# Expert results weighted on VectorE and scattered to rows by choice and token

## What is computed

```
gates = sum over both choices of one_hot(expert) * w_sel          # w_sel: softmax of the two, times p_group
acc   = acc + gate[:, e] * ((silu(t @ w1[e]) * (t @ w3[e])) @ w2[e])  # for e in 0..31
x     = x + g2 * acc                                              # g2: one row for context, one for latent tokens
y     = x * rsqrt(mean(x * x) + eps) * final_norm_g
```

## Time and profile before

| | |
|---|---|
| median of 3 runs | 724.87 us (724.36 to 725.55) |
| the profiled execution | 726.14 us, of which the span of the trace is 724.2 us |
| mean granted clock of TensorE | 0.922 |
| busy: PE, DVE, ACT, POOL | 597.5, 260.8, 165.0, 113.3 us |
| moved by DMA | 182.52 MB, 252 GB/s over the span |

### The profile page before, as it was taken

How to read it: one execution, slowest core, us unless ns; L and a number is a source line. 1 busy time by engine, 2 the same in 40 slices (tenths; PEclk the granted TensorE clock), 3 DMA queues, 4 the chain that set the end, 5 groups by cost and what they waited for, 6 DMA issues and landing times.

```text
span 724.2 us, 8452 instructions
## 1 busy us (share of the span) xinstructions
PE 597.5 (82%) x3472; PEld 396.5 (55%) x3472; DVE 260.8 (36%) x529; ACT 165.0 (23%) x306; POOL 113.3 (16%) x89
## 2 busy tenths in 40 slices
PE   3799999999999899999997469998888888787400
PEld 3579999888888644544554445554444444443100
DVE  1441248350504443515677627321111111111067
ACT  5333531122221322201111112111111111111143
POOL 0134623333332000010000011010000000000140
PEclk9899999999999999999999569999999999989855
DMA  7985133033032698379106829999999999998273
GB/s 284 387 305 175 40 117 117 0 117 115 2 117 81 245 354 307 119 257 350 60 30 251 330 78 377 423 422 421 422 419 423 419 421 420 422 423 347 63 276 145
DMA packets 50001, 182.52 MB, mean 252 GB/s; under 512 B 5445, under 2 KB 5493, under 8 KB 37161
## 3 DMA queue, kind: packets, MB, share of 16 engines
q1 hardware_dynamic: 37688, 150.78, 52.9%
q0 software_dynamic: 6192, 20.15, 7.8%
q10 hardware_dynamic: 6080, 11.02, 4.3%
HBM read 170.89 MB, written 14.19 MB: 256 GB/s over the span
## 4 chain that ended last, share of the span: by engine, by line
PE 63%; DMA 21%; DVE 7%; SPq 3%; ACT 3%; issue 2%; ACTq 0%; POOL 0%; DVEq 0%; POOLq 0%
DMA ring<-in_w_up_e 13%; PE bank L924 9%; PE bank L926 9%; PE bank L925 9%; PE bank L1094 9%; PE bank L1170 9%; DMA arena_ab<-in_w_up_e 5%; PE bank L1190 4%; PE bank L883 3%; DMA x<-in_x_sample 1%; PE bank L1111 1%; PE bank L1162 1%; SPq L447 1%; SPq L443 1%; PE bank L1044 1%
## 5 line engine op out<-in xcount | busy, mean ns | idle before, releaser
L1170 PE MATMUL bank<-ring,arena_ab 128*64 128x256 f32 x416 | 111.7, 430 | 30.1 <-DMA ring<-in_w_up_e 28.7
L1174 PE MATMUL bank<-ring,arena_ab 128*64 128x256 f32 x416 | 111.7, 430 | 0.0
L1170 PEld LDWEIGHTS bank<-ring,arena_ab 128*64 128x64 f32 x416 | 62.9, 155 | 83.0 <-DMA ring<-in_w_up_e 42.4
L1264 DVE TENSOR_TENSOR arena_ab<-arena_ab,bank 64x256 f32<-64x256 f32 x32 | 19.5, 610 | 193.1 <-ACT arena_ab L812 193.1
L533 POOL TENSOR_TENSOR w_lo<-ring,w_hi 128x1024 fp32r<-128x1024 f32 x25 | 61.3, 2454 | 112.5 <-ACT w_hi L672 112.5
L924 PE MATMUL bank<-xn_hi,w_hi 128*128 128x320 f32 x192 | 61.5, 320 | 3.2 <-DVE xn_lo L1264 3.1
L924 PE MATMUL bank<-w_hi,xn_hi 128*128 128x512 f32 x160 | 63.2, 395 | 0.0
L1174 PEld LDWEIGHTS bank<-ring,arena_ab 128*64 128x64 f32 x416 | 62.9, 155 | 0.0
L925 PE MATMUL bank<-w_lo,xn_hi 128*128 128x512 f32 x160 | 62.8, 393 | 0.0
L926 PE MATMUL bank<-w_hi,xn_lo 128*128 128x512 f32 x160 | 62.8, 392 | 0.0
L926 PE MATMUL bank<-xn_hi,w_lo 128*128 128x320 f32 x192 | 60.1, 313 | 0.0
(11 more groups left out here) (223 smaller groups left out, 873.4 us busy)
## 6 DMA issues: line engine op xcount, KB each, us to landing
ring<-in_w_gate_e SPq DMA_DIRECT2D x26, 1024.0 KB, 26.1
ring<-in_w_up_e SPq DMA_DIRECT2D x26, 1024.0 KB, 29.0
ring<-in_w_down_e SPq DMA_DIRECT2D x26, 1024.0 KB, 28.1
ring<-in_w_ada SPq DMA_DIRECT2D x11, 2048.0 KB, 12.2
ring<-in_w_in SPq DMA_DIRECT2D x6, 2048.0 KB, 8.4
expert_out_rows<-arena_ab ACTq DMA_DIRECT2D x64, 128.0 KB, 7.1
arena_ab<-in_w_gate_e SPq DMA_DIRECT2D x6, 1024.0 KB, 27.9
arena_ab<-in_w_up_e SPq DMA_DIRECT2D x6, 1024.0 KB, 30.5
```

Source lines behind the costliest of these rows:

```text
L1170: pe.matmul(bank[2 + p_][0:BLK, 0:DE], lhs, w_gate(s)[:, kt, :], start=(kt == 0), stop=(kt == KT - 1))
L1174: last = pe.matmul(bank[2 + p_][BLK:2 * BLK, 0:DE], lhs, w_up(s)[:, kt, :], start=(kt == 0), stop=(kt == KT - 1))
L1264: return dve.tensor_tensor(out, in0, in1, op)
```

## The change

The result of a slot is now weighted where it leaves PSUM, and only used slots are written, to a row that is the token's own.

- VectorE works out the weights right after the index list (`weights` before the first expert; the inputs of the exponentials are sent to ScalarE before the last `place`). `out_tags` writes for each token and expert a tag (token number, plus 640 for the second choice) and the weight. `out_table` on TensorE multiplies the one-hot slot matrices by these and so gets, for each slot, its destination row and its weight, apart for context and latent tokens. `out_rows` turns that into `row_out`, the list of half rows to write to (out of range for empty slots), and `g_ctx`, `g_lat`.
- For each expert VectorE's `gate_rows` makes a tile `gate_row` = g2 of the latent tokens times the slot's latent weight plus g2 of the context tokens times its context weight, and `results` multiplies the down product by it out of PSUM. ScalarE's `results` is gone.
- POOL scatters the tile by an indirect DMA to `half_rows`: 2 x 2 x 640 half rows of 512 numbers, by choice, token and half. A scatter waits for `y_ev`.
- In the tail SyncE loads both choices of a tile by two contiguous DMAs, `combine` is two sums, `first_part` is gone. The load of the final norm's weights stands behind the last scatter on POOL's queue.
- `result_rows` and its list are gone; the copy of g2 in SBUF is by halves (`second_gate`).

```diff
@@ def rows_back / gathers on POOL
             for q_ in range(PAIRS):
...
+            def result_rows_out(n, p_, column):
+                pool.wait_ge(y_ev, n + 1)
+                pool.indirect_dma_start(half_rows, bass.IndirectOffsetOnAxis(ap=column, axis=0), ysb[:, p_, :], None,
+                                        bounds_check=2 * 2 * TOK - 1, oob_is_err=False).then_inc(y_out[p_], 16)
+            for q_ in range(2):
+                gather_rows(q_, idx[:, q_:q_ + 1])
+            pool.wait_ge(row_out_ready, 1)
+            for m in range(PAIRS):
+                if m + 2 < PAIRS:
+                    pool.wait_ge(xe_mm, 2 * (m + 1))
+                    gather_rows(m % 2, idx[:, m + 2:m + 3])
+                for p_ in range(2):
+                    result_rows_out(2 * m + p_, p_, row_out[:, 2 * m + p_:2 * m + p_ + 1])
             pool.dma_start(g_fin, a["final_norm_g"].partition_broadcast(P)).then_inc(gfin_in, 16)
...
-            for t in range(NT):
-                for j in range(2):
-                    result_rows_in(t, j, y_rows[0:OV_ROW0, :], OV_ROW0 - 1).then_inc(got_in[t], 16)
@@ sync
             sp.sem_inc(y_all, 1)
+            for t in range(NT):
+                for j in range(2):
+                    sp.dma_start(got[:, t, j, :], y_rows[j * TOK + P * t:j * TOK + P * t + P, :]).then_inc(got_in[t], 16)
@@ scalar
-            def results(n, p_, stored_before):
-                act.wait_ge(down_mm, n + 1)
...
-                act.activation(ysb[:, p_, :], bank[6 + p_][:, :], ACT.Copy).then_inc(y_ev, 1)
...
-            def first_part(t):
-                act.wait_ge(got_in[t], 32)
-                act.activation(got[:, t, 0, :], got[:, t, 0, :], ACT.Copy, scale=wsel[:, t, 0:1]).then_inc(part0_ready, 1)
@@ tensor
+            def out_table():
+                pe.wait_ge(tags_ready, 1)
+                for t in range(NT):
+                    cols = slice(2 * EXPERTS * min(t, 1), 2 * EXPERTS * min(t, 1) + 2 * EXPERTS)
+                    for j in range(2):
+                        for half in range(2):
+                            last = pe.matmul(bank[6][BLK * half:BLK * half + BLK, cols], hit(t, j), tag_out[:, t, j, :],
+                                             start=(t < 2 and j == 0), stop=(t in (0, NT - 1) and j == 1))
+                last.then_inc(table_mm, 1)
+            out_table()
             def rows_T(p_, tiles):
...
                 pe.wait_ge(ht_ready, n + 1)
+                if n == 0:
+                    pe.wait_ge(row_out_ready, 1)
@@ vector
             choose(NT - 1)
+            tt(rt[:, 60:65], rt[:, 170:175], rt[:, 165:170], ALU.subtract).then_inc(exp_in, 1)
             place(NT - 1)
...
+            def gate_rows(p_, lat, ctx_):
+                then(dve.tensor_scalar(gate_row[:, p_, :], second_gate[:, 1, :], lat, None, ALU.mult))
+                then(dve.scalar_tensor_tensor(out=gate_row[:, p_, :], in0=second_gate[:, 0, :], scalar=ctx_, in1=gate_row[:, p_, :],
+                                              op0=ALU.mult, op1=ALU.add))
+            def results(n, p_):
+                dve.wait_ge(down_mm, n + 1)
+                if n >= 2:
+                    dve.wait_ge(y_out[p_], 16 * (n // 2))
+                tt(ysb[:, p_, :], bank[6 + p_][:, :], gate_row[:, p_, :], ALU.mult).then_inc(y_ev, 1)
...
             row_table()
-            tt(rt[:, 60:65], rt[:, 170:175], rt[:, 165:170], ALU.subtract).then_inc(exp_in, 1)
+            weights()
+            out_tags()
+            out_rows()
...
+                if n >= 1:
+                    results(n - 1, (n - 1) % 2)
+                gate_rows(n % 2, g_lat[:, n:n + 1], g_ctx[:, n:n + 1])
                 if n == 0:
                     overflow_counts()
-                elif n == 1:
-                    result_rows()
...
                 g0, g1 = got[:, t, 0, :], got[:, t, 1, :]
                 dve.wait_ge(got_in[t], 32)
-                dve.wait_ge(part0_ready, t + 1)
-                then(dve.scalar_tensor_tensor(out=g0, in0=g1, scalar=wsel[:, t, 1:2], in1=g0, op0=ALU.mult, op1=ALU.add))
-                then(tt(g0, g0, rows[3][:, min(t, 1), :], ALU.mult))
+                then(tt(g0, g0, g1, ALU.add))
                 tt(x[:, t, :], x[:, t, :], g0, ALU.add).then_inc(x2_ready[t], 1)
```

More of the change, by code:

```diff
@@ L1229, in _ @@
                 pe.wait_ge(ht_ready, EXPERTS)
+                pe.wait_ge(ov_tags_ready, 1)
+                for n in range(2 * NT):
+                    lo = 64 * (1 + min(n // 2, 1))
+                    for half in range(2):
+                        pe.matmul(bank[5][BLK * half:BLK * half + BLK, lo:lo + 2 * OVB], hit_ov[:, n, :], tag_ov[:, n, :],
+                                  start=(n in (0, 2)), stop=(n in (1, 2 * NT - 1)))
                 for n in range(2 * NT):
@@ new lines, in weights, with out_tags @@
+                then(tt(w_sel[:, :, 1], w, e21, ALU.mult))
+            def out_tags():
+                mine = b_ada_all[:, 128:128 + 2 * NT * EXPERTS].rearrange("p (t j n) -> p t j n", t=NT, j=2)
+                choices = [te(flat2(CHOICE[j])) for j in range(2)]
+                dve.tensor_copy(tag_out[:, :, 0, 0:EXPERTS], mine[:, :, 0, :])
+                dve.scalar_tensor_tensor(out=tag_out[:, :, 1, 0:EXPERTS], in0=choices[1], scalar=float(TOK), in1=mine[:, :, 1, :],
+                                         op0=ALU.mult, op1=ALU.add)
+                for j in range(2):
+                    last = tt(tag_out[:, :, j, EXPERTS:2 * EXPERTS], choices[j], over(w_sel[:, :, j], EXPERTS), ALU.mult)
+                last.then_inc(tags_ready, 1)
@@ new lines, in _ @@
+                ov(dve.scalar_tensor_tensor(out=tag_ov.rearrange("p (t j) b -> p t j b", j=2)[:, :, 1, 0:OVB],
+                                            in0=on.rearrange("p (t j) b -> p t j b", j=2)[:, :, 1, :], scalar=float(TOK), in1=second,
+                                            op0=ALU.mult, op1=ALU.add), 3)
+                tt(on, on, over(rt[:, 240:250], OVB), ALU.mult).then_inc(ov_tags_ready, 1)
+                dve.wait_ge(ov_slot_mm, 1)
+                token, none = rt[:, 300:300 + OVB // 2], rt[:, 320:320 + OVB // 2]
@@ L1705, in _ @@
+                ov(dve.tensor_copy(token, bank[4][:, 0:OVB // 2]), 4)
+                ov(dve.tensor_scalar(none, token, 0.0, float(FAR), ALU.is_equal, ALU.mult), 5)
                 dve.scalar_tensor_tensor(out=idx_ov[:, :], in0=token, scalar=-1.0, in1=none, op0=ALU.add,
                                          op1=ALU.add).then_inc(idx_ov_ready, 1)
[L1707 to L1713 removed]
+                dest, empty = rt[:, 340:340 + OVB], rt[:, 370:370 + OVB]
@@ L1716, in _ @@
+                dve.wait_ge(ov_rows_ready, 1)
             dve.wait_ge(gfin_in, 16)
-            dve.wait_ge(rows_in[3], 16)
             dve.wait_ge(routed, 1)
```

148 lines of the change are left out of this document (79 added, 69 removed).

## The result

The changed kernel took 716.04 us (median of 6 runs, 711.56 to 721.61) beside 725.53 us (6 runs) of the kernel before: ratio 0.9878, 95% interval 0.9833 to 0.9923, so 9.5 us faster. A later comparison gave 717.53 us (715.34 to 724.31) beside 726.31, ratio 0.9899 (0.9861 to 0.9938). The forecast was 713.8, with a range from 707.5 to 718.5.

A forecast was written before the change was run, and what follows sets the result against it. The prediction took the DMA engines as the bound from about 440 us, then one chain from the last expert to the end. Its terms, 0.2 + 0.3 - 3 - 8.6 = -11.1 us, took 724.87 to 713.8, range 707.5 to 718.5.

The forecast's parts named there:

- Start, +0.5 us in all: Start of the expert stage: +0.2 us for new weight and table work, +0.3 for two more VectorE operations at expert 0.
- rival 2: Start of the stage: the table takes 5 us, not hidden by the gather; +2 to +3 us, 716.5; chance 0.08.
- DMA-bound stretch, -3 us: Expert stage from about 440: writing only used slots relieves the slowest DMA engine; 3 us saved, bounds 0 and 7.
- rival 1: DMA-bound stretch: the scatter relieves all DMA engines alike, 7 us in place of 3, so 709.8; chance 0.18.
- the drain: End of the weights, as DMA engines finish at different times: up to 8 us before, 10 us or more forecast.
- the ring: Middle of the expert stage: loop of product, scatter, gather, transposes and down product, forecast at 16.1 us for two experts.
- Tail, -8.6 us: Behind the last expert: 2.1 us sooner to the first loaded results, then 6.5 us from one VectorE operation less per tile.
- rival 4: No effect in the middle and the final norm's weights late: 720; chance 0.14 together with the mild form.
- rival 3: Middle, on POOL: gathers wait behind scatters; mild 716 to 723 (0.14 together with rival 4), full 750 (0.05).
- That makes 16.1, below 17.2: Middle: loop of 5.6 us plus 10.5 for the gather's landing, compared with gathers 17.24 us apart before.
- the mild form: Rival 3 with a gather landing near 12 us: 716 to 723; chance 0.14 together with rival 4.
- backlog of the DMA queue: Middle: a later TensorE only shortens this backlog; with the loop as bound, the queue empties and landing falls towards 4.3 us.

The follow-up runs named there:

- the gathers ahead: Changed kernel with POOL issuing the gather of pair m+3 before the two scatters of pair m instead of behind them; 712.06 us, ratio 0.9819.
- all rows written: Kernel with the gathers ahead, each unused slot scattered to a spare row of its own instead of skipped; 714.41 us, ratio 0.9841.
- the spread: Kernel with the gathers ahead, consecutive slots dealt to partitions four apart; 705.63 us. Same edit in the kernel before 725.69, in the changed kernel 711.85.

## Why the prediction was right in its time and wrong in its path

**What bounds the kernel.** The DMA engines as the bound from 440 on: true before and with the gathers ahead (a share of 1.01 in 440 to 480 and 1.02 in 480 to 640 in both), not in the changed kernel (0.99 in 440 to 480, and 14 waits on gathered rows).

**Start, +0.5 us in all: nothing.** The table took 2.45 us (priced 2.6, 419.06 to 421.51) and was hidden by the gather. The index list ended 0.5 us sooner in this execution, at 417.24; counted from there the first copy of transposed rows came after 6.4 us, as in the earlier trace rows, and the first expert's gate and up products, at 425.31, after 8.1, as before. So rival 2 is out.

**DMA-bound stretch, -3 us: the size holds, the place does not.** The saved rows are worth 3.5 us of the weights' landing in one pair of profiles and 2.4 us of the medians once the weights are the bound (all rows written), so rival 1, with 7, is out. The slowest engine was the better choice than the mean byte: the spread, at the same bytes, brings the landing forward by another 4.1 us, and the drain with the gathers ahead is 13 us, longer than the 8 before, as the prediction said. That weights and old stores load all engines evenly rests on the mean share of 1.01 to 1.02 from 440 to 640, not on a view of each engine; with only the gathers' slots spread, in the kernel before, the drain went from 8 us to 3. In the time of the changed kernel none of the 3 us was seen, for TensorE had the ring to wait for.

**Tail, -8.6 us: right, a little small.** From the end of the last transposes to the end of the span 9.6 us went: 1.55 from ScalarE's hidden state (1.5 priced), 6.3 from the two sums per tile (6.5 priced), and 1.75 between the last product and the first sum (0.6 priced). There the scatter landed 2.4 us after POOL began it and not 4.3, and the first tile's loads took 6.9 us from the first issue, where 6.1 was priced with the norm's share. The first three final norms are 4.21 us apart, 5.53 before, the 1.3 closer that the prediction named. VectorE did not wait for the final norm's weights, so that half of rival 4 is out; its other half, no effect in the middle, is what came.

**The step that failed is rival 3's sum**, "That makes 16.1, below 17.2", by which the ring was set aside and the mild form got a part of 0.14. Three things were wrong in it.

First the comparison. 17.24 us is the pace of gathers after 488. Up to there the kernel before ran at 12.34 us a pair, and the ring held these early pairs back as well: its first three turns took 17.7, 18.0 and 16.8 us. The ends had to be compared, not two paces. First gather 449.55, 12 turns of 16.1, 9.9 for the last landing, and 25.2 from there to the end of the last down product (four experts at 6.17 and little else): 677.9. That is already 2 us later than the 675.9 which the forecast had for the last down product's end. With the measured 16.61 it is 684.0, the 683.98 of the trace, as it must be with all terms from there.

Second a term of the sum. The transposes and the down product were priced at 2.6 us, with the down product of the earlier trace rows, where the granted clock was 1.00 (678 to 680.5). In the ring they took 4.2 in the turn shown and 3.8 in the mean of 13, behind waits of TensorE. The gather was priced too high in return: it landed after 9.7 in the mean, not 10.5. With the other steps as measured (0.1 more) that makes 16.6 where 16.1 was forecast, so this term is worth less than the comparison. With a quick product the ring was 14.5 to 15.2 us long, and the same sum with 14.8 ends at 662, ahead of the 673.9 at which the weights let the last down product end with the gathers ahead; with the slow products the ring is the bound. That is worked out and was not run.

Third the argument that a shorter "backlog of the DMA queue" or an emptier queue would give the loss back. The DMA share in 440 to 480 fell only from 1.01 to 0.99, and a gather still took 9.5 us to land.

The price at a granted clock of 1.00 did not hold for most turns: it was 0.50 in 660 to 662 after no matmul in 656 to 658, and 0.51 to 0.65 over the slow products of the first profile, 0.50 to 0.64 over those of the second. But 2 of 13 turns in the first profile and 5 of 13 in the second had a quick product, at 1.00. A lower clock behind the waits was not weighed against rival 3.

So 716.04 came out where the tail's 9.6 is nearly all of the gain and the middle gave nothing, with 2.2 us between forecast and median, and a single execution anywhere from 711.6 to 724.3. That the time came so near is in part luck: the 3 us of the middle were missing, and 0.5 us of the start and 1.0 us of the tail came out better than priced. The forecast of 713.8 is nearly that of the kernel with the gathers ahead, 712.06, which has the path that the prediction described.

## What to carry to other kernels

When an instruction that waits for a result is put into an in-order queue ahead of the load of the next input, write down the ring that this closes and compare where it ends with where the other bound ends, not one pace with another. Price the compute inside a ring higher if the ring makes it wait: here its transposes and down product took 3.8 us in the mean where 2.6 was priced. Then issue the loads first: here that took 4 us off and brought the runs from 10 us apart to 2.4.

## What the hardware showed that was not expected

- A down product (8 matmuls in the rows) took 1.87 to 1.94 us behind other work, and 2.8 to 3.64 us in 32 of 39 turns of three profiles behind a wait for rows, of 2.2 to 5.0 us in these turns; the granted clock over these 32 products was 0.50 to 0.65, over the seven quick ones of the 39 turns 1.00.
- An indirect scatter of up to 128 rows of 2 KB took POOL 1.27 us to issue in the stage and 0.98 as the last one, and the rows of that last one landed 2.4 us after POOL began (2.39 to 2.41 in eight of ten profiles, 2.76 with all rows written, 2.96 with the final norm's weights loaded ahead).
- Which partitions hold the used slots is worth 6.4 us (0.9%) at the same bytes with the gathers ahead, and nothing in the time of the kernel before.
